# A two-layer encoder trunk on one core: the mixture-of-experts routing works on raw rows, in another order

## The reference, cut to what matters

```python
x = x + g1 * mixer(...)
h = rmsnorm(x, norm_ffn_g[l]) * (1 + sc2) + sh2
scores = sigmoid(h @ router_w)               # 512 x 16, router shared by the layers
biased = scores + router_bias
# best group of 4 by the sum of its two best; the two best experts inside it; weights are normed scores
x = x + g2 * experts(h)                      # blocks of 128 tokens, each block one expert
```

## Time and profile before

| what | us |
|---|---|
| median of 3 runs | 1453.41 |
| the profiled execution, its own time | 1452.14 |
| its span | 1450.4 |
| TensorE busy in the span | 1266.7 (87%) |
| VectorE busy | 943.0 (65%) |
| ScalarE busy | 594.2 (41%) |
| GpSimd busy | 171.7 (12%) |
| mean granted TensorE clock | 0.94 of full speed |

### The profile page before, as it was taken

How to read it: one execution, slowest core, us unless ns; L and a number is a source line. 1 busy time by engine, 2 the same in 40 slices (tenths; PEclk the granted TensorE clock), 3 DMA queues, 4 the chain that set the end, 5 groups by cost and what they waited for, 6 DMA issues and landing times.

```text
span 1450.4 us, 14168 instructions
## 1 busy us (share of the span) xinstructions
PE 1266.7 (87%) x4809; PEld 812.1 (56%) x4809; DVE 943.0 (65%) x1320; ACT 594.2 (41%) x794; POOL 171.7 (12%) x181
## 2 busy tenths in 40 slices
PE   2999899748999999983999999997389999999881
PEld 2544344436666666741788844466366666667430
DVE  8488974566777777614866588735667777776114
ACT  3265101335555555403322167633355555554001
POOL 6000001010000000002000057800110000000002
PEclk9999999859999999996999999998599999999995
DMA  9965585307999999874465410004679999998445
GB/s 353 373 206 186 168 297 204 144 30 293 364 368 367 364 378 386 303 288 138 158 242 179 141 58 1 1 15 160 257 275 374 378 361 370 380 365 306 147 172 188
DMA packets 79616, 353.13 MB, mean 243 GB/s; under 512 B 12697, under 2 KB 12881, under 8 KB 70609
## 3 DMA queue, kind: packets, MB, share of 16 engines
q1 hardware_dynamic: 67680, 327.28, 61.3%
q0 software_dynamic: 8352, 20.46, 3.9%
q10 hardware_dynamic: 3536, 4.79, 0.9%
HBM read 334.15 MB, written 28.31 MB: 250 GB/s over the span
## 4 chain that ended last, share of the span: by engine, by line
PE 77%; DVE 13%; DMA 3%; ACT 3%; issue 2%; POOL 1%; SPq 0%; DVEq 0%; POOLq 0%; ACTq 0%
PE ps L1680 24%; PE ps L1691 17%; PE ps L1779 8%; PE ps L1582 6%; PE ps L1614 4%; PE ps L1671 3%; PE ps L1621 3%; DVE scratch L945 2%; PE ps L1666 2%; PE ps L1823 2%; PE ps L1851 2%; PE ps L1837 2%; DMA slab_ring<-in_mod_w_dram 1%; PE ps L1685 1%; PE ps L1545 1%
## 5 line engine op out<-in xcount | busy, mean ns | idle before, releaser
L1691 PE MATMUL ps<-slab_ring,scratch 128*128 128x512 f32 x560 | 246.5, 593 | 3.4 <-ACT scratch L853 2.1
L1680 PE MATMUL ps<-slab_ring_r,gate_rows_r 128*128 128x512 f32 x512 | 202.4, 395 | 0.0
L1691 PEld LDWEIGHTS ps<-slab_ring,scratch 128*128 128x128 f32 x560 | 105.8, 190 | 124.2 <-issue 117.3
L1334 DVE TENSOR_TENSOR slab_ring_r<-slab_ring,h_t_r 128x2048 fp32r<-128x2048 f32 x64 | 143.8, 2288 | 22.7 <-ACT h_t_r L805 22.6
L1582 PE MATMUL ps<-h_t,slab_ring 128*128 128x512 f32 x320 | 142.1, 603 | 0.0
L1779 PE MATMUL ps<-slab_ring_r 128*128 128x512 f32 x384 | 121.2, 397 | 2.7 <-DVE h_t_r L1002 2.7
L1680 PE MATMUL ps<-h_t_r,gate_rows_r 128*128 128x512 f32 x256 | 106.2, 415 | 14.7 <-DVE scratch_r L1328 7.4
L805 ACT ACTIVATE h_t_r<-slab_ring 128x2048 fp32r<-128x2048 f32 x64 | 118.4, 1901 | 0.2 <-issue 0.2
L1680 PEld LDWEIGHTS ps<-slab_ring_r,gate_rows_r 128*128 128x128 f32 x512 | 98.3, 192 | 19.3 <-issue 0.5
L1582 PEld LDWEIGHTS ps<-h_t,slab_ring 128*128 128x128 f32 x320 | 62.1, 195 | 78.3 <-issue 77.7
L794 ACT ACTIVATE scratch<-ps,mod_ab 128x128 f32<-128x128 f32 x128 | 48.1, 457 | 135.8 <-PE ps L1666 135.8
(11 more groups left out here) (300 smaller groups left out, 2116.4 us busy)
## 6 DMA issues: line engine op xcount, KB each, us to landing
slab_ring<-in_expert_w_gate_dram SPq DMA_DIRECT2D x35, 2048.0 KB, 9.8
slab_ring<-in_expert_w_up_dram SPq DMA_DIRECT2D x35, 2048.0 KB, 9.9
slab_ring<-in_expert_w_down_dram SPq DMA_DIRECT2D x35, 2048.0 KB, 10.0
mod_ring<-in_mod_w_dram SPq DMA_DIRECT2D x48, 512.0 KB, 4.6
y_rows<-scratch SPq DMA_DIRECT2D x35, 512.0 KB, 10.5
slab_ring<-in_mod_w_dram SPq DMA_DIRECT2D x32, 512.0 KB, 4.6
slab_ring<-in_w_qkv_dram SPq DMA_DIRECT2D x6, 2048.0 KB, 11.5
slab_ring<-in_w_in_ab_dram SPq DMA_DIRECT2D x5, 2048.0 KB, 14.6
```

Of the source, the lines that this page charges most:

```text
L1334: tt_(rest, w, top.bitcast(F32), ALU.subtract).then_inc(low_ready[c], 1)
L1680: ins = pe.matmul(ps[:, bank, :], x, w, start=(kt == 0 and i == 0), stop=(kt == KT - 1 and i == 2))
L1691: ins = pe.matmul(ps[:, 5 + h, :], hidT[:, f, :], w[:, 2 * f + h, :], start=(f == 0), stop=(f == FT - 1))
```

## The change

1. In the routing stages TensorE transposes the raw residual rows (`turn_x` waits for `x_ready`) and plain copies of them (`XT`, two buffers) meet router weights that already carry the scale; the shift's share is one small product per layer. The logits are multiplied by the inverse root on VectorE afterwards (`scale_logits`).
2. `project` runs in pieces: kt 0 to 2 of half 0, transposes of t-1, kt 3 to 5, logits of t-1, kt 6 and 7, then half 1. The residual is added per half.
3. The split of expert 0's gate weights moves into the tile loop on ScalarE and VectorE. Expert 0's slots come from its ranks alone (`place_first`), block 0 is gathered on them, and info and weights are made in the first expert's step (`route_rest`). Blocks 0 and 1 are gathered without the copy of their index.
4. The zeros are stored right after the first transposes; ScalarE waits for them at input tile 8, VectorE no longer does. In the head one reciprocal serves all four tiles.
5. Attention's probabilities, the output slabs and their high and low parts change slabs; in layer 1 the first gate slab now waits for the last attention product and the first up slab for `y_ready` 15.

```diff
@@ stream_experts @@
-                    1: [(y_ready, 16), (y_ready, 16), (y_ready, 16), (av_ready, 8), (y_ready, 16), (y_ready, 16)]}[l]
+                    1: [(av_ready, 8), (y_ready, 15), (y_ready, 16), (y_ready, 16), (y_ready, 16), (y_ready, 16)]}[l]
@@ SP, before layer 1's experts @@
-        sp.wait_ge(qkv_ready, 20)
+        sp.wait_ge(qkv_ready, 24)
         load_slab(("o", 0), w_o[:, :, 0:HALF])
-        sp.wait_ge(qkv_ready, 24)
+        sp.wait_ge(mod_used, LAYERS * PARTS * MOD_SLICES)
@@ GpSimd @@
-        zeros = R[:, 8:10, :].rearrange("p a n -> p (a n)")
-        gp.wait_ge(scan_done, LRU_TILES)
+        zeros = XN[:, 0, :]
+        gp.wait_ge(xn_turned, TT)
         link(gp.memset(zeros, 0.0))
-        gp.wait_ge(y_ready, 1)
         for b in range(NE, NBLK):
             gp.dma_start(y_dram[b * P:(b + 1) * P, :], zeros).then_inc(y_zeroed, 16)
-        gp.wait_ge(y_zeroed, 16 * MAX_OVER)
...
-            gather(0, 0, xs_filled[0])
-            gather(1, 1, xs_filled[1])
+            gather_first(0, xs_filled[0])
+            gp.wait_ge(slots_ready, 2 * l + 2)
+            gather_first(1, xs_filled[1])
@@ ScalarE @@
+            if t == 8:
+                act.wait_ge(y_zeroed, 16 * MAX_OVER)
...
+            for t in range(TT):
+                square(s, t)
+                take_xt(t)
+                root(s, t)
+                act.wait_ge(xn_ready, TT * s + t + 1)
+                act.dma_start(xn_dram[t * P:(t + 1) * P, :], xnorm[s][:, t, :]).then_inc(xn_stored, 16)
+                act.wait_ge(logit_scaled, TT * l + t + 1)
+                act.activation(rt[:, t * NE:(t + 1) * NE], rt[:, t * NE:(t + 1) * NE], ACT.Sigmoid).then_inc(score_ready, 1)
+                if t in (1, 2):
+                    high(0, 0, 0, 0, t - 1, True)
@@ VectorE, head @@
-            v.wait_ge(rms_ready, t + 1)
-            v.reciprocal(stats[:, 2, t:t + 1], stats[:, 1, t:t + 1]).then_inc(x_inverse, 1)
+            if t == 0:
+                v.wait_ge(rms_ready, TT)
+                v.reciprocal(stats[:, 2, :], stats[:, 1, :]).then_inc(x_inverse, 1)
@@ VectorE, routing @@
+        def place_first(l):
+            v.wait_ge(rank_ready, l + 1)
+            link(stt(first_rank[:, :], hot[:, :, 0], -float(PAST), v3(ps[:, 1, 0:n])[:, :, 0], ALU.mult, ALU.add))
+            link(ts(first_rank[:, :], first_rank[:, :], float(PAST), None, ALU.add))
+            tt_(first_hot, p_id[:, :].unsqueeze(1).to_broadcast([P, TT, P]), first_rank[:, :].unsqueeze(2).to_broadcast([P, TT, P]), ALU.is_equal).then_inc(place_ready, 1)
+            v.wait_ge(slots_summed, 2 * l + 1)
+            found = ps[:, 2, 0:1]
+            link(ts(empty[:, 0:1], found, 0.0, float(NO_TOKEN), ALU.is_equal, ALU.mult))
+            stt(slot_tok[:, 0:1], found, -1.0, empty[:, 0:1], ALU.add, ALU.add).then_inc(slots_ready, 1)
...
+            def take_xt(t):
+                v.wait_ge(xn_turned, TT * s + t + 1)
+                if t >= 2:
+                    v.wait_ge(logit_ready, TT * l + t - 1)
+                v.tensor_copy(XT[t % 2][:, 4:8, :], ps[:, 2 * t + 1, :].rearrange("p (k n) -> p k n", n=P)).then_inc(ht_dve, 1)
+            def scale_logits(t):
+                cut = slice(t * NE, (t + 1) * NE)
+                v.wait_ge(logit_ready, TT * l + t + 1)
+                if t == 0:
+                    link(v.tensor_copy(shift_row[:, :], ps[:, 0, TT * NE:(TT + 1) * NE]))
+                stt(sc[:, cut], ps[:, 0, cut], stats[:, 2, t:t + 1], shift_row[:, :], ALU.mult, ALU.add).then_inc(logit_scaled, 1)
...
             for t in range(TT + 1):
+                if t:
+                    take_xt(t - 1)
+                    if t in (3, 4):
+                        low(0, 0, 0, t - 3)
+                    scale_x(s, t - 1)
+                    scale_logits(t - 1)
+                    choose(l, t - 1)
                 if t < TT:
                     residual(l, t)
+                    if t == 0:
+                        if l == 0:
+                            mod_take(MOD_SPLIT - 1)
+                        fold_router()
+            place_first(l)
             route(l)
@@ TensorE @@
-                project(l, t, 0)
+                project(l, t, 0, 0, 3)
                 if t:
                     turn_x(s, t - 1)
-                project(l, t, 1)
+                project(l, t, 0, 3, 6)
+                if t:
+                    logits(t - 1)
+                project(l, t, 0, 6, KT)
+                project(l, t, 1, 0, KT)
                 if l == 0 and t == 0:
                     mod_reduce(MOD_SPLIT - 1)
-                if t:
-                    logits(t - 1)
             turn_x(s, TT - 1)
             logits(TT - 1)
...
-            pe.wait_ge(place_ready, l + 1)
+            pe.wait_ge(place_ready, 2 * l + 1)
+            for t in range(TT):
+                ins = pe.matmul(ps[:, 2, 0:2], first_hot[:, t, :], tok_pair[:, t, :], start=(t == 0), stop=(t == TT - 1))
+            ins.then_inc(slots_summed, 1)
+
+            pe.wait_ge(place_ready, 2 * l + 2)
```

More of the change, by code:

```diff
@@ L175, in build @@
     rb = small("router_b", [P, NE])
+    shift_sum = small("router_shift_sum", [P, NE])
+    shift_row = small("router_shift_row", [P, NE])
+    tok_pair = small("token_id_pair", [P, TT, 2], F32R)
+    first_rank = small("first_rank", [P, TT])
     lru = small("lru_consts", [P, 6, 8])
@@ L791, in xst @@
                     act.wait_ge(up_done, e + (e0 - 1))
+                if first and par:
+                    act.wait_ge(route_ready, l + 1)
                 act.wait_ge(xs_turned, e + (e0 + 1))
@@ L827, in step @@
                     xst(e + 1, 1 - par, first == 1)
-            for chunk in range(2):
-                high(0, 0, 0, 0, chunk, True)
             xst(0, 0, True)
@@ L1191, in residual @@
         def residual(l, t):
-            v.wait_ge(y_ready, 8 * l + 2 * t + 2)
-            link(tt_(pair(2 * t), pair(2 * t), G[:, 2 * l, :], ALU.mult))
-            tt_(X[:, t, :], pair(2 * t), X[:, t, :], ALU.add).then_inc(x_ready, 1)
+            for h in range(2):
+                cut = slice(h * HALF, (h + 1) * HALF)
+                v.wait_ge(y_ready, 8 * l + 2 * t + h + 1)
+                link(tt_(ps[:, 2 * t + h, :], ps[:, 2 * t + h, :], G[:, 2 * l, cut], ALU.mult))
+                ins = tt_(X[:, t, cut], ps[:, 2 * t + h, :], X[:, t, cut], ALU.add)
+            ins.then_inc(x_ready, 1)
             v.wait_ge(x_ready, TT * 2 * l + t + 1)
@@ L1350, in step @@
                     low(1, e, par, chunk)
+                if first:
+                    route_rest(l)
                 if not last:
@@ L1360, in step @@
                 tt_(hid, ps[:, 3, :], sg, ALU.mult).then_inc(hid_ready, 1)
-            for chunk in range(2):
-                low(0, 0, 0, chunk)
             xst(0, 0, True)
@@ L1606, in _, with project @@
                 mod_reduce(reduce_after[t])
-        def project(l, t, half):
+        def project(l, t, half, first, end):
             cut = slice(t * P, (t + 1) * P)
@@ L1612, in project @@
                 wait_slab(pe, ("out", half))
-                for i, kt in enumerate((4, 5, 6, 7, 0, 1, 2, 3)):
+                for i in range(first, end):
+                    kt = (i + 4) % KT
                     ins = pe.matmul(ps[:, 2 * t + half, :], mixT[:, kt, cut], slab(("out", half))[:, kt, :], start=(i == 0), stop=(i == KT - 1))
@@ L1616, in project @@
                 top, rest = ring_r[:, WO_HIGH_SLOT[half], :, :], ring_r[:, place["o", half][0], :, :]
-                for kt in range(KT):
+                for kt in range(first, end):
                     if t == 0 and kt % (KT // WO_CHUNKS) == 0:
```

133 lines of the change are left out of this document (75 added, 58 removed).

## The result

The changed kernel takes 1439.99 us (median of 4 runs, 1439.51 to 1441.09), the kernel before 1453.82 us in the same comparison: a ratio of 0.9913 with a 95% interval of 0.9895 to 0.9930, or 13.8 us less, under 1% and clear of no change. The profiled execution took 1440.28 us with a span of 1438.5; before it was 1452.14 with 1450.4.

A forecast was written before the change was run, and what follows sets the result against it. TensorE bounds most of the span (77%); gains lie in stretches where it does not. 1452.14 - 20.5 (routing stages) + 5.3 (head) = 1436.9 profiled, median 1.3 higher, so 1438 us; range 1428 to 1445.

The forecast's parts named there:

- Up to the ranks: Routing up to tile 3's choice, timed from P, the last projected half tile's end: 5.8 and 6.2 us gained by layer.
- The cold case: Routing with TensorE's clock at the low level: logits 3.58 us, tile 3 chosen 7.6 after its ready row.
- After the ranks, layer 0: From R, VectorE's first step on the ranks, to `turn_xs`: R + 10.25 instead of R + 13.9, gaining 3.65 us.
- After the ranks, layer 1: Layer 1, from the ranks to `turn_xs`: R + 11.1 instead of R + 15.9, gaining 4.8 us, bounds 3.3 to 5.6.
- the last store, issued 9 us before the gather, lands in time even at 7.6: Layer 1: the last store of normed rows, at most 7.6 us long, would not hold up block 0's gather.
- The gather's own 8: Layer 1: block 0's gather, with five 2 MB loads in flight, takes 8 us, bounds 6.55 and 4.49 + 5.0.
- The head: Kernel start and first mixer: reduction of part 1 2.9 us earlier, zero fill delays part 2; net 5.3 us late.
- the 8.5: Head: the zero fill's toll on the loads of part 2's slices, 8.5 us, bounds 0 and 9.0.
- absorb 2.0: First mixer: two existing waits of 1.0 each, VectorE's for ScalarE and the second tile's gates for TensorE, shorten the delay.
- The 2.9 of the earlier head: Head: TensorE's reduction of part 1 starts 2.9 us earlier, at about 35.3 instead of 38.23, but this is lost.
- The stretches that I left at nothing: Places assumed to cost nothing, such as changed slabs and later output-weight loads, first used tens of us later under attention.
- hidden fill: Head: SP's packets win over the zero fill, part 2 starts at 72.64 as before, total 1430 us; chance 0.22.

The follow-up runs named there:

- the last three runs: Changed kernel with transposes waiting for the normed row, 1475.95 us; the same for tile 3 only, 1444.80 us; projection in whole halves, 1455.86 us.
- the transposes first: Changed kernel with expert 0's eight transposes ahead of TensorE's eight slot-table products, and VectorE's table reading later: 1438.61 us.
- the late fill: Changed kernel with its zero fill held back until part 2's eight slices have been taken: 1430.25 us.
- held loads: Changed kernel with the three loads of layer 1's expert 1 held back until expert 0's gather has landed: 1438.58 us.
- all three together: Changed kernel with the zero fill late, layer 1's expert 1 loads held back, and expert 0's transposes ahead of the table's products: 1425.14 us.
- the early fill with four reciprocals: Changed kernel with its early zero fill kept and one reciprocal for each tile again: 1443.69 us.

## Why the prediction was right, and where it was off

By the profiled executions it had 15.2 us less, and 11.9 came.

*Up to the ranks.* Forecast: choice of tile 3 at P + 8.6 and P 1.8 later in layer 0, 5.8 gained; measured P + 8.4, P 2.0 later, 5.8 gained. In layer 1, 6.2 forecast, 6.1 measured (72.57 to 66.51 from the first projected half to the ranks). The cold case was the one that came: the logits took 3.57. What this stands on is the pair that the last three runs take apart: the raw rows, worth 3.9 us up to the ranks in layer 0 and 3.4 in layer 1, and the pieces, without which VectorE's order puts tile 2's choice in the way. ScalarE had its root 1.29 us after the start of the table load again (290.74 and 292.03), and the sigmoid as soon after its own, so the drain of the Trainium skill (ScalarE: Activation LUTs, What ACT_TABLE_LOAD costs) does not show in the changed kernel either.

*After the ranks, layer 0.* Forecast `turn_xs` at R + 10.25, measured R + 9.95. "The gather leaves the path and `route` takes its place" is borne out: the gather landed 7.7 us after R (forecast 7.6), and half a microsecond ahead of VectorE's last table, in the changed kernel and with the transposes first.

*After the ranks, layer 1.* Forecast 4.8 gained, measured 3.35 to the first product. The step that failed is "the last store, issued 9 us before the gather, lands in time even at 7.6". It took 11.2 us and held the gather for 2.2 us past its slots; I had taken the longest store of the earlier trace rows as a bound. Loads stood around that store too, five of 2 MB, against four here, so their number doesn't say why this one took longer; that stays open. The gather's own 8 was near (7.05). The term was mis-sized, at the low bound that I had given (3.3).

*The head.* The first slice of part 2 was forecast for 81.1 and came at 81.24; the fill took the 8.1 to 8.7 us of each 3.67 MB from the loads, as the rule on queues (the Trainium skill, DMA: Bandwidth & Descriptors, Issuing engines are not separate DMA queues) and the earlier trace rows said; the 8.5 was near. What failed is the step behind it: "absorb 2.0". The gates start 8.3 late, not 7.2: before, the waits between the first slice and the gates were 1.78 us (0.52, 0.63 and 0.63), not the 1.25 that I counted and took away, and 1.46 of waits stayed. The first projection is 7.8 late, not 5.3. I had followed VectorE and ScalarE alone. TensorE's reduction of part 2 stands in its queue ahead of the sixteen products and the gate product. Before, it started at 89.54 with no wait; now it waited 7.50 us for VectorE's sum and started 6.1 later. Behind that wait the clock was low (0.50 granted from 94 to 98 us, 1.00 in the kernel before), the four matmuls took 3.75 us instead of 1.88, and the gate product came at 106.18, 8.1 after the 98.12 of before. VectorE's 1.0 wait for ScalarE did go, as forecast. But ScalarE waited 2.84 us for the second tile's gate product, as in the earlier trace rows, and 8.05 later: the delay ran through TensorE past the slack. So the late sum is 6.1 of it, and the low clock 2.0, a term that the sum did not have. The 2.9 of the earlier head, 2.6 as it came, were counted as lost, and rightly: with the early fill TensorE waits them away at the reduction of part 2. With the late fill, 2.0 of them reach the first projection.

*The rest.* The stretches that I left at nothing gave -0.5 in sum. That is in part luck: without the 1.7 us of the clock's form in the last stretch the traces would lie 10.2 apart, against the 15.2 forecast.

The rival "hidden fill" had 1430 us as its time; the late fill gave 1430.25, but only its total is right, by chance: in that trace the two stages gave 19.6 us for its 20.5 and the head 0.1 for its 2.6, and 2.0 came from the last stretch in its fast form. No fill at all was not tried: it would leave the rows of unused overflow blocks unwritten.

## What to carry to other kernels

A transfer whose wait costs nothing still has a price: put it where no load is being waited for, and count its bytes against the load queue's next landing, not against its own deadline. When a wait is added to an in-order queue, first count what stands behind it: one line ahead of the transposes was 3.9 us of layer 0 on the last tile and 36 us in all when it also stood in the middle of the projections. And a step that now comes earlier meets other traffic: the longest store of the trace before is no bound for it. Last, when a change makes TensorE wait longer, price what runs behind that wait at the low clock too.

## What the runs showed of the hardware that was not expected

A 512 KB store took 2.6 us to land with no weight load in flight, 3.2 in layer 1 with one expert's loads held back, and 11.2 in the changed kernel with four loads of 2 MB in flight or queued. The number of loads is not all, for in the kernel before, with five, it took 7.6. The gather of 128 rows took 4.00, 4.49, 6.55, 7.05 and 7.36 us in these traces. The early slots issue it at R + 5.4 in layer 1 instead of R + 8.9, and TensorE's transposes come only 0.4 earlier against the ranks; two loads were then in flight with it instead of one.

TensorE's clock gives gains back. The same last overflow products of layer 1, with the same data, took 15.7 us in one trace and 14.0 in the other, and the rows of the two windows (the kernel before, then the changed one) have 0.83 and 1.00 as the granted clock:

```profile
1390.00:1400.00 10.00, 8.14 (x21) 3.81 (x20) 2.56 (x6) 1.50 (x4) 0.00 (x0) 0.83 0.78 261
```

```profile
1380.00:1390.00 10.00, 8.13 (x25) 4.00 (x24) 2.56 (x6) 1.50 (x4) 0.00 (x0) 1.00 0.79 262
```

That is the table's last 1.7 us, and the run with held loads had the slow form again (products in 15.7 us). Of the fourteen traces four have it: the kernel before, held loads, all three together, and the early fill with four reciprocals. The kernel before with the early fill has the fast one. Nothing that the change does touches this stretch, so it is no gain of the change; what decides between the two forms was not found.
